# Opening of a two-block transformer kernel: another order of the first transfers, of the filter network and of one product

## The reference

```python
silu_c, silu_cc = jax.nn.silu(c), jax.nn.silu(c_ctx)
sh1, sc1, gt1, sh2, sc2, gt2 = jnp.split((silu_c @ ada_w[layer] + ada_b[layer])[:, None, :], 6, axis=-1)
csh1, csc1, ... = jnp.split(silu_cc @ ada_w[layer] + ada_b[layer], 6, axis=-1)
h = modulate(rms_norm(x, norm1_g[layer]), sh1, sc1)          # h * (1 + scale) + shift
hc = modulate(rms_norm(ctx, norm1_g[layer]), csh1, csc1)
q, k, v, g, hy_u, gate_ret, gate_hy = jnp.split(h @ w_in[layer] + b_in[layer], IN_SPLITS, axis=-1)

# hyena_filters: a small network over positions gives the filters of a long convolution
hid = jnp.sin(freq * (feats @ w1 + b1))
hid = jnp.sin(freq * (hid @ w2 + b2))
filt = hid @ w3
filt = filt * jnp.exp(-t[:, None] * deltas[None, :])
filt = filt / jnp.sum(jnp.abs(filt), axis=0, keepdims=True)
```

## Time and profile before

| | us |
|---|---|
| median of 3 runs (1876.67 to 1880.20) | 1877.49 |
| the profiled execution | 1879.73 |
| its span | 1878.0 |
| TensorE busy (matmuls) in the span | 1778.8 |
| VectorE busy | 465.8 |
| ScalarE busy | 318.5 |

### The profile page before, as it was taken

How to read it: one execution, slowest core, us unless ns; L and a number is a source line. 1 busy time by engine, 2 the same in 40 slices (tenths; PEclk the granted TensorE clock), 3 DMA queues, 4 the chain that set the end, 5 groups by cost and what they waited for, 6 DMA issues and landing times. The chain is left out here.

```text
span 1878.0 us, 24533 instructions
## 1 busy us (share of the span) xinstructions
PE 1778.8 (95%) x10834; PEld 1350.2 (72%) x10834; DVE 465.8 (25%) x1014; ACT 318.5 (17%) x722; POOL 0.2 (0%) x4
## 2 busy tenths in 40 slices
PE   5999999998998899999999999899999999899997
PEld 3675887886663566666766677688888876788886
DVE  4411225434024221111101245422100134411001
ACT  4110013112214111000000124321100134111000
POOL 0000000000000000000000000000000000000000
PEclk9999999999999999999999999899999999999999
DMA  9353666557799999999999952187644131354430
GB/s 380 156 224 127 237 234 239 196 201 304 286 417 375 381 421 411 420 421 422 421 420 421 414 188 90 51 332 280 234 157 156 69 113 64 121 207 149 155 112 23
DMA packets 61378, 470.84 MB, mean 251 GB/s; under 512 B 7543, under 2 KB 11032, under 8 KB 11864
## 3 DMA queue, kind: packets, MB, share of 16 engines
q1 hardware_dynamic: 60184, 467.98, 64.0%
q10 hardware_dynamic: 1088, 1.28, 0.2%
HBM read 468.19 MB, written 1.05 MB: 250 GB/s over the span
## 5 line engine op out<-in xcount | busy, mean ns | idle before, releaser
L2393 PE MATMUL bank<-hT,ring 128*128 128x256 f32 x1024 | 222.5, 379 | 0.0
L2416 PE MATMUL bank<-second_work,ring 128*128 128x256 f32 x1024 | 221.3, 379 | 0.0
L2416 PEld LDWEIGHTS bank<-second_work,ring 128*128 128x128 f32 x1024 | 194.6, 190 | 26.5
L2393 PEld LDWEIGHTS bank<-hT,ring 128*128 128x128 f32 x1024 | 194.3, 190 | 26.0
L1282 PE MATMUL bank<-hT,ring 128*128 128x256 f32 x672 | 152.9, 384 | 8.2 <-DMA ring<-in_w_ff 5.4
L1282 PEld LDWEIGHTS bank<-hT,ring 128*128 128x128 f32 x672 | 126.7, 191 | 40.9 <-DMA ring<-in_w_ff 12.4
L603 PE MATMUL bank<-hT,ring 128*128 128x256 f32 x704 | 153.5, 379 | 0.0
L603 PEld LDWEIGHTS bank<-hT,ring 128*128 128x128 f32 x704 | 133.5, 190 | 18.9 <-issue 1.2
L1713 PE MATMUL bank<-ring,rowsT 128*32 128x512 f32 x1024 | 120.0, 603 | 0.3
L1282 PE MATMUL bank<-tmp,ring 128*128 128x256 f32 x384 | 87.2, 382 | 7.6 <-DMA ring<-in_w_ff 6.6
L1282 PEld LDWEIGHTS bank<-tmp,ring 128*128 128x128 f32 x384 | 71.7, 190 | 27.3 <-DMA ring<-in_w_ff 13.7
(11 more groups left out here) (458 smaller groups left out, 1686.2 us busy)
## 6 DMA issues: line engine op xcount, KB each, us to landing
ring<-in_expert_w SPq DMA_DIRECT2D x192, 1024.0 KB, 12.6
ring<-in_w_ff SPq DMA_DIRECT2D x96, 1024.0 KB, 5.4
ring<-in_ada_w SPq DMA_DIRECT2D x36, 2048.0 KB, 8.5
ring<-in_w_in SPq DMA_DIRECT2D x27, 1024.0 KB, 8.3
ring<-in_w_in SPq DMA_DIRECT2D x13, 2048.0 KB, 10.9
ring<-in_w_out SPq DMA_DIRECT2D x12, 1024.0 KB, 5.9
ring<-in_ret_w_o SPq DMA_DIRECT2D x2, 2048.0 KB, 8.2
ring<-in_w_out SPq DMA_DIRECT2D x2, 2048.0 KB, 12.6
```

The lines of the kernel that those rows point to most:

```text
L2393: mm = pe.matmul(ff_bank(n), w[:, k, (n % 2) * P:(n % 2 + 1) * P], hT[:, k, xs], start=k == 0, stop=k == DT - 1)
L2416: mm = pe.matmul(ff_bank(FT + i), w[:, f, :], W[:, 16 * h + f, :], start=h == f == 0, stop=h == 1 and f == FT // 2 - 1)
```

## The change

Everything is in the first stage. Line numbers of the kernel after differ by up to 3.

**Transfers.** SP starts with chunk 0 and xT, then layer 3's weights, chunk 1, the decay table, chunks 2 and 3. ScalarE issues the conditioning vectors, the four small loads of the filter network, the decay row, `base`, `cols` and the router's bias.

```diff
--- before.py
+++ after.py
@@ -561,10 +561,6 @@
                             pe.wait_ge(S("hy_sin"), 1)
                             pe.matmul(bank[1][0:HY_FFN, 0:T], hy_w2, hid[0:HY_FFN, :], start=True, stop=True)\
                                 .then_inc(S("hy_mm"), 1)
-                            pe.wait_ge(S("x_sq_added"), 3)
-                            pe.matmul(bank[6][:, 0:T], ones[:, :], hT[:, 0, xs], start=True, stop=True).then_inc(S("x_sum"), 1)
-                            pe.wait_ge(S("base_loaded"), 16)
-                            ada.pe(pe, 1)
 
                             pe.wait_ge(S("hy_sin"), 2)
                             pe.wait_ge(S("hy_w3_loaded"), 16)
@@ -574,8 +570,11 @@
                                     pe.matmul(bank[2 * t + h][:, :], hid[:, t * P:(t + 1) * P],
                                               hy_w3[:, h * HY:(h + 1) * HY], start=True, stop=True)\
                                         .then_inc(S("hy_mm"), 1)
+                            pe.wait_ge(S("base_loaded"), 16)
+                            ada.pe(pe, 1)
+                            pe.wait_ge(S("x_sq_added"), 3)
+                            pe.matmul(bank[6][:, 0:T], ones[:, :], hT[:, 0, xs], start=True, stop=True).then_inc(S("x_sum"), 1)
                             ada.pe(pe, 2)
-                            ada.pe(pe, 3)
 
                             pe.wait_ge(S("hy_mag"), 4)
                             pe.wait_ge(S("x_root"), 1)
@@ -584,6 +583,7 @@
                                     mm = pe.matmul(bank[6 + h][:, :], ones[:, :], mag[:, 2 * t + h, :], start=t == 0,
                                                    stop=t == TT - 1)
                                 mm.then_inc(S("hy_l1"), 1)
+                            ada.pe(pe, 3)
 
                             seen = set()
                             for i, (c, last, products, shape) in enumerate(tiles):
@@ -627,12 +627,11 @@
 
                         @block.sync
                         def _(sp):
-                            sp.dma_start(hy_w1, a["hy_w1"]).then_inc(S("mlp_loaded"), 16)
-                            sp.dma_start(feats, a["feats"]).then_inc(S("mlp_loaded"), 16)
-                            sp.dma_start(hy_w2, a["hy_w2"]).then_inc(S("mlp_loaded"), 16)
-                            sp.dma_start(hy_vec, a["hy_vec"]).then_inc(S("mlp_loaded"), 16)
                             load_ahead(sp, -1, 1)
                             sp.dma_start(xT[:, :, :], a["xT"]).then_inc(S("x_loaded"), 16)
+                            sp.dma_start(hy_w3[0:HY_FFN, :], a["hy_w3"]).then_inc(S("hy_w3_loaded"), 16)
+                            load_ahead(sp, -1, 2)
+                            sp.dma_start(early[:, 2 * 512:], a["early"][:, 2 * 512:]).then_inc(S("hy_decay_loaded"), 16)
                             load_ahead(sp, -1, ADA0)
                             load_ahead(sp, at["ada"][0], in0[0] + 1)
                             sp.dma_start(cT[:, :, :], a["ctxT"]).then_inc(S("ctx_loaded"), 16)
@@ -715,23 +714,23 @@
                             do(nc.vector.tensor_tensor(la, la, x, ALU.min), "lg_neg")
                             dve.wait_ge(S("mlp_loaded"), 64)
                             layer_input(0)
-                            quarter_sum(hT[:, :, xs], "x_sq", 2, "x_sq_added")
-                            layer_input(1)
                             dve.wait_ge(S("lg_exp"), 1)
                             do(nc.vector.tensor_scalar(la, la, 1.0, None, ALU.add), "lg_one")
                             do(nc.vector.tensor_scalar(log_g[:, :], x, 0.0, None, ALU.min))
-                            dve.wait_ge(S("x_root"), 1)
-                            do(nc.vector.reciprocal(rstd[:, xs], rstd[:, xs]))
-                            dve.wait_ge(S("lg_ln"), 1)
-                            do(nc.vector.tensor_tensor(log_g[:, :], log_g[:, :], lb, ALU.subtract))
-                            dve.wait_ge(S("cols_loaded"), 16)
-                            ada.dve(dve, 1)
+                            layer_input(1)
+                            quarter_sum(hT[:, :, xs], "x_sq", 2, "x_sq_added")
                             dve.wait_ge(S("hy_decay_loaded"), 16)
                             for t in range(TT):
                                 for h in range(2):
                                     dve.wait_ge(S("hy_mm"), 3 + 2 * t + h)
                                     do(nc.vector.tensor_tensor(filt[:, 2 * t + h, :], bank[2 * t + h][:, :],
                                                                E1("hy_decay", t * HY, HY), ALU.mult), "hy_filt")
+                            dve.wait_ge(S("cols_loaded"), 16)
+                            ada.dve(dve, 1)
+                            dve.wait_ge(S("lg_ln"), 1)
+                            do(nc.vector.tensor_tensor(log_g[:, :], log_g[:, :], lb, ALU.subtract))
+                            dve.wait_ge(S("x_root"), 1)
+                            do(nc.vector.reciprocal(rstd[:, xs], rstd[:, xs]))
                             ada.dve(dve, 2)
                             ada.dve(dve, 3)
                             dve.wait_ge(S("first_added"), ADA0)
@@ -789,12 +788,14 @@
                                         .then_inc(S(done), 1)
 
                             act.dma_start(conds[:, :, :], a["conds"]).then_inc(S("conds_loaded"), 16)
+                            act.dma_start(hy_w1, a["hy_w1"]).then_inc(S("mlp_loaded"), 16)
+                            act.dma_start(feats, a["feats"]).then_inc(S("mlp_loaded"), 16)
+                            act.dma_start(hy_w2, a["hy_w2"]).then_inc(S("mlp_loaded"), 16)
+                            act.dma_start(hy_vec, a["hy_vec"]).then_inc(S("mlp_loaded"), 16)
                             act.dma_start(row("decay"), a["rows"][:, QK_W + V_W:].to_broadcast([P, 2 * HEADS]))\
                                 .then_inc(S("decay_loaded"), 16)
                             act.dma_start(base[:, :], a["base"]).then_inc(S("base_loaded"), 16)
                             act.dma_start(cols[:, :], a["cols"]).then_inc(S("cols_loaded"), 16)
-                            act.dma_start(hy_w3[0:HY_FFN, :], a["hy_w3"]).then_inc(S("hy_w3_loaded"), 16)
-                            act.dma_start(early[:, 2 * 512:], a["early"][:, 2 * 512:]).then_inc(S("hy_decay_loaded"), 16)
                             act.dma_start(router_b[:, :], a["router_rows"].to_broadcast([P, GROUPS + EXPERTS]))\
                                 .then_inc(S("router_b_loaded"), 16)
 
@@ -813,11 +814,13 @@
                             do(nc.scalar.activation(hid[0:HY_FFN, :], arg, ACT.Sin), "hy_sin")
                             act.wait_ge(S("lg_one"), 1)
                             do(nc.scalar.activation(lb, la, ACT.Ln), "lg_ln")
-                            root(bank[6], xs, "x_sum", "x_root")
-                            ada.act(act, 1)
                             for n in range(4):
                                 act.wait_ge(S("hy_filt"), n + 1)
                                 do(nc.scalar.activation(mag[:, n, :], filt[:, n, :], ACT.Abs), "hy_mag")
+                                if n == 0:
+                                    ada.act(act, 1)
+                                if n == 1:
+                                    root(bank[6], xs, "x_sum", "x_root")
                             ada.act(act, 2)
                             ada.act(act, 3)
                             act.wait_ge(S("first_mod"), 1)
```

## The result

The changed kernel is slower. In the first comparison its median was 1888.81 us (1882.39 to 1890.09, 5 runs) against 1877.49 (1873.49 to 1880.20, 5 runs): ratio 1.0061, interval 1.0041 to 1.0081. Single executions of either kernel spread over 12 us, so this ratio is not the last word. In the three comparisons the means differ by 10.3, 12.4 and 6.8 us. Over all of them the mean of 21 runs of the changed kernel is 1885.4 and that of 77 runs of the kernel before 1876.3: 9.1 us, 0.5%. This 9.1 depends on which runs are taken together: 29 of the 77 ran on a chip on which the changed kernel did not, and without them it is 8.6. The profiled execution took 1887.22 with a span of 1885.4, against 1879.73 and 1878.0.

A forecast was written before the change was run, and what follows sets the result against it. TensorE was taken as busy nearly everywhere except the first slice, with later loads following it. Units +4.9 and cooled tiles +1.3 gave +6.2 on the median 1877.49: 1883.7, forecast 1883.5 us, range 1876.0 to 1888.0.

The forecast's parts named there:

- A shift of the projection passes one to one to the end: Behind the opening: later loads are issued when TensorE frees slots, so everything moves by the same amount as the input projection.
- A small row costs a large row of waiting: Opening loads: the two DMA queues take turns row by row; beside chunk 0 a turn costs 0.63 us. Chance 0.58.
- The first rival: Opening loads: small loads keep ahead of the bulk, filter loads in by 6.5, units -2.6, time 1876.2 us; chance 0.17.
- The decay row lands at 16.5 (13.3 to 19.6): ScalarE's queue: the decay row, which layer 1 on VectorE waits for, lands at 16.5 us, the middle of its bounds.
- two counts, 27 turns and 36: Decay row's wait per engine: 27 turns (10.6 us), or 36 (13.8 us) if the conditioning's 9 have not slipped through before.
- two overheads, 1.9 and 5.1: Start and completion time added to the decay row's turns: 1.9 us from the conditioning, 5.1 us from chunk 0.
- the check: Row turns tried on the decay table's landing in the kernel before: 16.4 us computed, 15.1 measured.
- The rival with a backlog: Opening loads: decay row handed out only after xT's and chunk 1's rows, landing nearer 20, +9.7, 1887.2 us; chance 0.10.
- The chain from there to the units, 28.8 us: Opening, from the decay row's landing at 16.5 through layers, Abs, L1 product and chunk 3 to units at 45.3: +4.9.
- The first tiles cooled, +1.3: First projection tiles: TensorE idles about 2.8 us before L610, and the lowered clock behind that adds 1.3 us.
- The sum: Whole kernel: +4.9 to the units and +1.3 for the stall's clock make +6.2 us.

The follow-up runs named there:

- the run with 8 KB rows: Changed kernel with chunk 0 loaded as two transfers of 8 KB rows instead of one of 16 KB rows; ratio to the kernel before 1.0036 (1.0011 to 1.0062).
- the third trace: Trace of the changed kernel run a third time, no edit; ratio to the kernel before 1.0037 (1.0020 to 1.0053).
- the second comparison: The changed kernel once more, no edit, against the kernel before; ratio 1.0082 (1.0066 to 1.0099).
- decay row first: Changed kernel with the decay row issued by SP ahead of chunk 0, not by ScalarE behind the filter loads; ratio to the kernel before 1.0017 (1.0001 to 1.0033).

## Why the prediction was right or wrong, by its steps

- **A shift of the projection passes one to one to the end**: right up to 400 us in every trace (8.26 at every matmul in the first). Behind it single traces of the kernels tried, set against the one trace of before, win back up to 8.5 us or add up to 2.5. So it is shown less sharply that the shift arrives at the end whole: the openings differ by 9.0, the means of the three comparisons by 10.3, 12.4 and 6.8. That the mean over all runs, 9.1, lies so near to 9.0 is luck.
- **A small row costs a large row of waiting**: right, and shown by the packets (618 against 620) and by the run with 8 KB rows. The first rival, with the filter loads in by 6.5, is out: L556 came at 16.3 to 16.65. The Trainium skill ("DMA: Bandwidth & Descriptors", Queues, rings and completion order), which leads to that rival, has an engine drain a packet of about 9 to 17 descriptors of one queue row before it switches. These traces agree with the taking of turns and not with that size: one row of data at a time from each queue.
- **The decay row lands at 16.5 (13.3 to 19.6)**: this is the step that failed. It landed at 3.54 + 16.3 = 19.8. Of the two counts, 27 turns and 36, and of the two overheads, 1.9 and 5.1, I took the middle; my reason, that the check errs both ways, does not stand, since I had one check, the decay table, and it came out 1.3 too late. The conditioning did not slip through (8.2 us from issue to landing), so it was 36 turns. The landings agree: the row landed between chunk 1 (2.25 + 16.9 = 19.2) and the decay table (3.11 + 17.5 = 20.6), where 36 turns end. In time the 13.8 us for 36 turns were short. From 10 to 14 us the engines moved 272 GB/s, not 423; by my estimate, 4 x (1 - 272/423), that is 1.4 us. The rest of the shortfall is not resolved by term.
- **The rival with a backlog** (decay row nearer 20, sum +9.7) came nearer in numbers than my forecast: 19.8 and +9.0. Its mechanism is not what happened. It had the decay row's rows handed out only after those of xT and chunk 1; but from 3 to 19 us ScalarE's queue got as many turns as SP's, 620 and 618, so it never stood back. 36 turns, some of them slow, do it without a backlog.
- **The chain from there to the units, 28.8 us**: right. Measured 48.66 - 19.84 = 28.8 with layer 3 at 5.73 (taken: 5.5). From the decay row's first instruction the three traces give 28.5 to 29.5, nearly all of the difference from layer 3's clock (5.50 to 6.77).
- **The first tiles cooled, +1.3**: wrong in place. TensorE did drop to 1.2 GHz, not at the wait for L610 but before it, at 51 us (granted 0.66 over 50 to 55) behind the 1.9 idle before the units, and the two tiles took 8.83 instead of 7.07. It cost nothing: VectorE's queue sets L610, and TensorE still waited 0.49 for it. In the third trace the tiles ran warm, 7.14, and the wait was 2.18, with L610 10.55 behind the units' start in both. Nor did a wait of 2.18 slow what stands behind it: the distance to the trace of before stays at 8.66 up to 400 us.
- **The sum**: +6.2 forecast, +9.0 in the openings (+8.3 between the two profiled traces): +3.3 from the decay row, -1.3 from the cooling, +0.7 because the trace of before was itself late by 0.7 against the mean of its three. So side and mechanism held, and the term that was mis-sized is the landing of the decay row. With +9.0 alone the time would have been 1886.5, inside the range; the median was 1888.81, above its end of 1888.0. The 2.3 us between them do not lie in the opening, and their cause is open. They may be spread, but the second comparison had more of them (12.4) and only the third, with the most runs, less (6.8). I had made the range from the bounds of the terms and put the scatter of the times at nothing: the median of the kernel before alone was anywhere between 1872.76 and 1877.75 in four sets of runs.

## What to carry to other kernels

In this kernel small loads belong ahead of the first large one, also of one that another engine issues: beside it each of their rows waited for a large row, whatever its own size (12 bytes to 1 KB), and what waits for the last of them waits for all. When a transfer is moved to the front to start sooner, first count the rows of the small ones that it will now stand beside, and ask which engine's queue holds on to each. A quarter of a per cent in a kernel whose executions spread by 12 us is read from the marks of the traces, not from five times.

## What was not expected of the hardware

The conditioning (issued 0.72) and chunk 0 (0.73) were issued 0.01 us apart, yet from 1.5 to 2.8 us the engines started 16 packets of chunk 0 and none of ScalarE's queue:

```profile
q1 hardware_dynamic: 16, 0.26, 104.3%
```

With chunk 0 in front the 16 KB landed after 8.2 us, with a small load in front on SP's queue after 1.9 (before) and 3.3 (decay row first). How much of this is the order in front and how much the half microsecond by which chunk 0 then came later was not tried apart.

The stretch from 10 to 14 us, with busy engines at 272 GB/s, is unexplained; with 8 KB rows it is there too (292 GB/s).

And two traces of the same program, with openings 0.4 us apart, ended 7.0 us apart (spans 1885.4 and 1878.4). The stretches at 1.2 GHz behind 400 us are a part of it at most: between 400 and 800 us the granted clock was 0.97 and 0.98, a difference of some 4 us at full clock, while the first trace came about 1 us nearer to the trace of before and the second about 9. What places them in one execution and not in another was not tried.
